# Gate and up of a routed expert with the weights stationary and 96 gathered tokens moving

## The chip, the cores and the metric

The kernel runs on one core of a Trainium2 chip. The metric is the device time of one execution in microseconds (us). The engines that matter are TensorE (PE, with its weight loads shown apart as PEld), VectorE (DVE), ScalarE (ACT) and SyncE (SP), which issues the DMAs.

## The reference

A decoder trunk of two layers runs over 256 tokens of width 1024, in float32. Layer 0 is an attention and retention mixer and a dense SwiGLU; layer 1 is another mixer and a mixture of eight experts, of which each token takes two. The change lies in the experts:

```python
logits = (xf @ router).astype(jnp.float32)            # 256 x 8
top_logits, top_idx = lax.top_k(logits, TOP_K)        # TOP_K = 2
gates = jax.nn.softmax(top_logits, axis=-1)
...
def expert_block(args):
    xb, e = args
    return (jax.nn.silu(xb @ w_gate[e]) * (xb @ w_up[e])) @ w_down[e]
```

`w_gate` and `w_up` are 1024 x 3584 for each expert and `w_down` is 3584 x 1024. The 256 tokens make 512 routed rows, 64 for an expert on the mean. With the reference's own default inputs its routing gives the eight experts 49, 66, 46, 70, 69, 61, 86 and 65 tokens.

## The kernel before

**Three products for one.** Each operand of a large product is split into a rounded part (`_hi`, type float32r) and the rest (`_lo`). `mm3` (lines 262 to 266) issues three matmuls into the same bank: hi x hi, hi x lo or lo x hi, and the other. The first operand of `mm3` is the stationary one, which a weight load puts into the array; the second one moves, at most 512 columns.

**Units.** Weights come in units of 128 x 1024 elements. SP loads two units at a time (1 MB) into one of 14 ring slots (`m_load`, line 1266). ACT rounds a unit into one of four buffers `w_hi` (`hi_unit`, line 273), DVE takes the rest into `w_lo` (`lo_unit`, line 277), and PE reads both. ACT may fill a buffer only when PE has finished the unit four before it (`unit_used`), and PE waits for `split_ready`, which DVE raises.

**Experts.** `moe_pe`, `moe_act`, `moe_dve` and `moe_sp` each loop over the eight experts. The hidden width of 3584 is cut into NFC = 7 chunks of 512. A chunk has 12 units: four of gate, four of up and four of down, so an expert has 84 and the eight have 672. PE's order in a chunk c from 1 on is gate(c), the turning of chunk c-1, up(c), down(c-1); gate and up of chunk 0 stand at the end of the expert before.

**Gathering.** For each expert `gather_pe` (line 1318) multiplies the normalised rows `xn` with a matrix `pick` of zeros and ones. That gives the expert's tokens transposed, with the width on the partitions: eight blocks of 128 x CAP, CAP = 128 being the number of places. ACT and DVE split them into `xe_hi` and `xe_lo`.

**Gate and up** (`gate_up`). The gathered tokens (128 x 128) are stationary and 512 columns of the weights move:

```python
for kk in range(2):
    k = 4 * plan[m][2] + 2 * u + kk
    w = slice(kk * 512, kk * 512 + 512)
    ins = mm3(bank, xe_hi[:, k, :], xe_lo[:, k, :], w_hi[:, buf, w], w_lo[:, buf, w],
              k == 0, k == KD - 1)
```

That is 6 matmuls for a unit. The product has the tokens on the partitions and the hidden width along the bank. ACT takes the silu of the gate (`silu_`, line 1347), DVE multiplies by up (`product`, line 1402), and since down contracts over the hidden width, `turn` transposes the result in four blocks on PE (line 1489) into bank 6. ACT rounds it (`turned`, line 1351) and DVE takes the rest (`rest`, line 1406).

**Down** (`down`). The turned block `hT` (128 x 128) is stationary and 512 columns of `w_down` move, 6 matmuls for a unit, summed over the chunks in banks 4 and 5. At the end of an expert the result is scaled by the gate and put back to its tokens by `scatter` (lines 1511 and 1512), and DVE adds it to `h` (line 1422).

**Order around the end of an expert.** On PE it is up(6), down(5), turning, the next expert's gather, down(6), gate(0) of the next expert, scatter, up(0).

**More tokens than places.** `overflow` reads the fullest expert's count on every engine, and if it is over CAP it runs the whole expert pass once more for the next CAP places.

**The dense SwiGLU of layer 0** is not touched. It has its weights stationary and 256 tokens moving (`f_gate_up`).

Of the kernel before, what the change touches and what calls it, by code (L numbers as in the profile page):

```python
# [26 lines left out]
P = 128  # L27
# [23 lines left out]
CAP = 128  # L51
# [17 lines left out]
def moe_items():  # L69
# [9 lines left out]
    ident=128, g_ab=8, eps=8, incl=128, negones=128, ones=128, before=128, strict=128, iota=256, cos_m=64, sin_m=64,  # L79
# [10 lines left out]
def trunk(nc, x, consts, decay_t, ab_w_in, w_uq, w_ukv, ab_w_out, f_gate, f_up, f_down,  # L90
          cd_w_in, cd_w_out, router, m_gate, m_up, m_down, moe_gain, final_gain, out):
    with ExitStack() as ctx:
# [70 lines left out]
        hT_lo = place("hT_lo", [P, 4, CAP], F32R, at=ARENA + 6144)  # L163
        g_moe_row = place("g_moe_row", [P, D], at=XT_AT + 12288)
        y_hi = place("y_hi", [P, D], F32R, at=ARENA + 8192)
        y_lo = place("y_lo", [P, D], F32R, at=XT_AT + 4096)
# [18 lines left out]
        def sem(name):  # L185
# [41 lines left out]
        prep_done, gather_banked, gather_hi, gathered, pgt_banked, pgt_done, e_silu, e_prod, h_banked, \  # L227
            hT_done, hT_lo_done, y_done, sc_banked, sc_done = (
                sem("e_" + n) for n in ("prep", "gather_banked", "gather_hi", "gathered", "pgt_banked",
                                        "pgt_done", "silu", "prod", "h_banked", "hT", "hT_lo", "y",  # L230
# [1071 lines left out]

        def gather_act(act, r, q):
            act.wait_ge(gather_banked, 2 * q + (r + 1))
            nc.scalar.activation(xe_hi[:, 4 * r:4 * r + 4, :].rearrange("p k t -> p (k t)"), pb[2 + r],
                                 ACT.Copy).then_inc(gather_hi, 1)

        def gather_dve(dve, r, q):
            dve.wait_ge(gather_hi, 2 * q + (r + 1))
            nc.vector.tensor_tensor(xe_lo[:, 4 * r:4 * r + 4, :].rearrange("p k t -> p (k t)"), pb[2 + r],  # L1310
                                    f32(xe_hi[:, 4 * r:4 * r + 4, :].rearrange("p k t -> p (k t)")),
                                    ALU.subtract).then_inc(gathered, 1)

        def gather_pe(pe, r):
            for kk in range(4):
                k = 4 * r + kk
                for tb in range(TB):
                    ins = nc.tensor.matmul(pb[2 + r][:, kk * P:kk * P + P], xn[:, tb, k * P:k * P + P],  # L1318
                                           pick[:, tb, :], start=tb == 0, stop=tb == 1)
            ins.then_inc(gather_banked, 1)  # L1320
# [21 lines left out]
        def moe_act(act, part):  # L1342
            def silu_(c, q):
                act.wait_ge(*m_used("g", c, q))

                act.wait_ge(h_banked, 7 * q + max(c, 1))
                nc.scalar.activation(eh[c % 2], pb[2 * (c % 2)], ACT.Silu).then_inc(e_silu, 1)

            def turned(c, q):
                act.wait_ge(h_banked, 7 * q + (c + 2))  # L1350
                nc.scalar.activation(hT_hi.rearrange("p j t -> p (j t)"), pb[6], ACT.Copy).then_inc(hT_done, 1)

            def outputs(q):
                act.wait_ge(*m_used("d", LAST, q))
                act.wait_ge(sc_done, 4 * q + 4)
                act.wait_ge(pgt_done, q + 1)
                for n in range(2):
                    nc.scalar.activation(y_hi[:, n * 512:n * 512 + 512], pb[4 + n], ACT.Copy,
                                         scale=place_gate).then_inc(y_hi_done, 1)

            def expert(e, q, last):
                for c in range(1, NFC):
                    m_hi(act, ("g", c), q)
                    m_hi(act, ("u", c), q)
                    turned(c - 1, q)
                    if c == 1:
                        act.wait_ge(pgt_banked, q + 1)

                        nc.scalar.activation(gate_sums, pb[7][:, 0:256], ACT.Copy,
                                             accum_out=place_gate).then_inc(pgt_done, 1)  # L1370
# [3 lines left out]
                turned(LAST, q)  # L1374
# [12 lines left out]
            q0 = NE * part  # L1387
            if part:
                m_hi(act, ("g", 0), q0)
            for r in range(2):  # L1390
                gather_act(act, r, q0)
            m_hi(act, ("u", 0), q0)
            silu_(0, q0)
            with act.Fori(0, NE - 1) as e:
                expert(e, e + q0, False)
            expert(NE - 1, q0 + NE - 1, True)

        def moe_dve(dve, part):
            def product(c, q):
                dve.wait_ge(*m_used("u", c, q))  # L1400
                dve.wait_ge(e_silu, 7 * q + (c + 1))
                nc.vector.tensor_tensor(eh[c % 2], eh[c % 2], pb[2 * (c % 2) + 1], ALU.mult).then_inc(e_prod, 1)

            def rest(c, q):
                dve.wait_ge(hT_done, 7 * q + (c + 1))
                nc.vector.tensor_tensor(hT_lo.rearrange("p j t -> p (j t)"), pb[6],  # L1406
                                        f32(hT_hi.rearrange("p j t -> p (j t)")),
                                        ALU.subtract).then_inc(hT_lo_done, 1)

            def outputs_rest(q):  # L1410
                for n in range(2):
                    w = slice(n * 512, n * 512 + 512)
                    dve.wait_ge(y_hi_done, 2 * q + (n + 1))
                    ins = nc.vector.scalar_tensor_tensor(out=y_lo[:, w], in0=pb[4 + n], scalar=place_gate,
                                                         in1=f32(y_hi[:, w]), op0=ALU.mult, op1=ALU.subtract)
                ins.then_inc(y_done, 1)
# [7 lines left out]
            def expert(e, q, last):  # L1424
                for c in range(1, NFC):
# [8 lines left out]
                    if c == 1:  # L1434
                        dve.wait_ge(pgt_done, q + 1)
                        nc.vector.tensor_scalar(pickT.rearrange("p b t -> p (b t)"), pb[7][:, 0:256], 0.0, None,
                                                ALU.is_gt).then_inc(pickT_done, 1)
# [34 lines left out]
        def moe_pe(pe, part):  # L1472
            def gate_up(kind, c, q):
                bank = pb[2 * (c % 2) + (kind == "u")]
                for m, u, n, buf in m_units((kind, c)):
                    pe.wait_ge(split_ready, UPE * q + (U_MOE + n + 1))
                    for kk in range(2):
                        k = 4 * plan[m][2] + 2 * u + kk
                        w = slice(kk * 512, kk * 512 + 512)
                        ins = mm3(bank, xe_hi[:, k, :], xe_lo[:, k, :], w_hi[:, buf, w], w_lo[:, buf, w],  # L1480
                                  k == 0, k == KD - 1)
                    ins.then_inc(unit_used, 1)

            def turn(c, q):
                pe.wait_ge(e_prod, 7 * q + (c + 2))
                if c:
                    pe.wait_ge(hT_lo_done, 7 * q + c)
                for j in range(4):
                    ins = nc.tensor.transpose(pb[6][:, j * P:j * P + P], eh[c % 2][:, j * P:j * P + P],  # L1489
                                              const("ident"))  # L1490
                ins.then_inc(h_banked, 1)

            def down(c, q):
                pe.wait_ge(hT_lo_done, 7 * q + (c + 1))
                if c == 0:
                    pe.wait_ge(y_done, q + 1)
                for m, u, n, buf in m_units(("d", c)):
                    t = 2 * plan[m][2] + u
                    pe.wait_ge(split_ready, UPE * q + (U_MOE + n + 1))
                    for nn in range(2):  # L1500
                        w = slice(nn * 512, nn * 512 + 512)
                        ins = mm3(pb[4 + nn], hT_hi[:, t, :], hT_lo[:, t, :], w_hi[:, buf, w],
                                  w_lo[:, buf, w], c == 0 and t == 0, c == LAST and t == 3)
                    ins.then_inc(unit_used, 1)

            def scatter(q):
                pe.wait_ge(y_done, q + 2)
                pe.wait_ge(pickT_done, q + 1)
                for s in range(4):
                    w = slice((s % 2) * 512, (s % 2) * 512 + 512)  # L1510
                    nc.tensor.matmul(pb[SC_BANKS[s]], pickT[:, s // 2, :], y_hi[:, w], start=True, stop=False)  # L1511
                    nc.tensor.matmul(pb[SC_BANKS[s]], pickT[:, s // 2, :], y_lo[:, w], start=False,  # L1512
                                     stop=True).then_inc(sc_banked, 1)

            def expert(q, last):
                for c in range(1, NFC):
# [4 lines left out]
                    turn(c - 1, q)  # L1521
                    if c == 1:
                        pe.wait_ge(prep_done, 2 * q + 2)
                        for tb in range(TB):
                            ins = nc.tensor.transpose(pb[7][:, tb * P:tb * P + P], pick_g[:, tb, :],
# [4 lines left out]
                turn(LAST, q)  # L1530
# [121 lines left out]
        def overflow(eng, body):  # L1652
# [3 lines left out]
            with eng.If(most > CAP):  # L1656
                body(eng, 1)
# [123 lines left out]
        def _(pe):  # L1781

            pe.sem_inc(unit_used, NBUF)
            pe.sem_inc(h_banked, 1)
# [17 lines left out]
        def _(dve):  # L1802
# [3 lines left out]
            dve.sem_inc(e_prod, 1)  # L1806
            dve.sem_inc(sc_done, 4)
# [34 lines left out]
def shape_tables(np):  # L1842
# [11 lines left out]
    t["iota"] = np.broadcast_to(np.arange(256, dtype=f), (P, 256))  # L1854
# [63 lines left out]
```

## Time and profile before

| | before |
|---|---|
| times of two runs | 1677.81 and 1678.82 us, median 1678.32 |
| span of the profiled execution | 1677.2 us, 0.6 and 1.6 us under the two times |
| PE busy | 1608.9 us (96%) |
| PEld busy | 1368.3 us (82%) |
| DVE busy | 1263.4 us (75%) |
| ACT busy | 1115.4 us (67%) |
| DMA | 444.35 MB, mean 265 GB/s |

The span runs from the first instruction to the last. Busy time of matmuls is longer than the step from one start to the next, since matmuls are pipelined and their ends are modelled: the price of a matmul in a stream is read from the starts in the timeline. PEclk is the clock granted to TensorE as a share of 2.4 GHz: 1.00 is 2.4 GHz, 0.50 is 1.2 GHz. The experts take the stretch from about 657 us to 1662 us.

### The profile page before, as it was taken

How to read it: one execution, taken by the hardware profiler on the slowest of the kernel's cores; microseconds unless marked ns; L12 is line 12 of the kernel's file. 1: busy time of each engine (PE TensorE's matmuls, PEld its weight loads, DVE VectorE, ACT ScalarE, POOL GpSimd, SP SyncE). 2: the span in 40 equal slices, each digit the busy share in tenths (PEclk: the TensorE clock that was granted, in tenths of full speed). 3: DMA queues.
4: the chain of work that ended last, by engine and by line, in shares of the span. 5: the costliest groups of instructions: out<-in, count | busy, mean ns of one | idle time of the engine just before them, and what ended most of it. 6: DMA issues, size and time to landing. Idle time of an engine off the chain costs nothing.

```text
span 1677.2 us, 23757 instructions
## 1 busy us (share of the span) xinstructions
PE 1608.9 (96%) x8136; PEld 1368.3 (82%) x8136; DVE 1263.4 (75%) x1430; ACT 1115.4 (67%) x1348; POOL 0.2 (0%) x4
## 2 busy tenths in 40 slices
PE   7988989999998998999999999999999999999995
PEld 6867789999898777888888888888888888888884
DVE  4446554445554556998998999999999999999995
ACT  5534454444365864887787787887877877877874
POOL 0000000000000000000000000000000000000000
PEclk9996999999998788999999999999999999999998
DMA  9630355554356054999999999999999999999950
GB/s 327 197 129 1 118 184 180 196 176 150 137 167 236 1 206 159 349 387 329 354 380 329 349 382 331 355 369 339 352 379 322 371 370 319 364 379 321 376 202 27
DMA packets 190916, 444.35 MB, mean 265 GB/s; under 512 B 7952, under 2 KB 25232, under 8 KB 190608
## 3 DMA queue, kind: packets, MB, share of 16 engines
q1 hardware_dynamic: 190864, 443.68, 73.6%
q8 instruction: 29, 0.48, 0.1%
q14 instruction: 23, 0.19, 0.0%
HBM read 442.61 MB, written 1.05 MB: 265 GB/s over the span
## 4 chain that ended last, share of the span: by engine, by line
PE 93%; DVE 3%; ACT 2%; issue 1%; DMA 0%; DVEq 0%; ACTq 0%; SPq 0%
PE bank L264 28%; PE bank L266 27%; PE bank L265 27%; PE bank L1318 2%; PE bank L1489 1%; PE bank L537 1%; PE bank L431 1%; PE bank L528 1%; PE bank L833 0%; ACT p_sb L593 0%; PE bank L1511 0%; PE bank L840 0%; PE bank L1512 0%; PE bank L527 0%; PE bank L418 0%
## 5 line engine op out<-in xcount | busy, mean ns | idle before, releaser
L277 DVE TENSOR_TENSOR w_lo<-ring,w_hi 128x1024 fp32r<-128x1024 f32 (+2 forms) x844 | 1004.9, 1208 | 272.2 <-ACT w_hi L273 233.1
L273 ACT ACTIVATE w_hi<-ring 128x1024 fp32r<-128x1024 f32 (+2 forms) x844 | 881.4, 1049 | 399.9 <-PE bank L266 398.5
L264 PE MATMUL bank<-w_hi,xe_hi 128*128 128x512 f32 x896 | 354.4, 396 | 1.4 <-DVE xe_lo L1310 1.4
L266 PE MATMUL bank<-w_hi,xe_lo 128*128 128x512 f32 x896 | 350.3, 391 | 0.0
L265 PE MATMUL bank<-w_lo,xe_hi 128*128 128x512 f32 x896 | 349.1, 390 | 0.0
L264 PEld LDWEIGHTS bank<-w_hi,xe_hi 128*128 128x128 f32 x896 | 168.3, 188 | 37.2 <-DVE w_lo L277 1.9
L266 PEld LDWEIGHTS bank<-w_hi,xe_lo 128*128 128x128 f32 x896 | 168.2, 188 | 36.3
L265 PEld LDWEIGHTS bank<-w_lo,xe_hi 128*128 128x128 f32 x896 | 168.4, 188 | 34.1
L264 PE MATMUL bank<-w_hi,hT_hi 128*128 128x512 f32 x448 | 177.9, 397 | 1.4 <-DVE hT_lo L1406 1.4
L266 PE MATMUL bank<-w_hi,hT_lo 128*128 128x512 f32 x448 | 176.9, 395 | 0.0
L265 PE MATMUL bank<-w_lo,hT_hi 128*128 128x512 f32 x448 | 176.8, 395 | 0.0
L264 PE MATMUL bank<-xT_hi,w_hi 128*128 128x256 f32 x448 | 127.0, 284 | 0.0
L265 PE MATMUL bank<-xT_lo,w_hi 128*128 128x256 f32 x448 | 126.9, 283 | 0.0
L266 PE MATMUL bank<-xT_hi,w_lo 128*128 128x256 f32 x448 | 126.8, 283 | 0.0
L264 PEld LDWEIGHTS bank<-w_hi,hT_hi 128*128 128x128 f32 x448 | 84.4, 188 | 20.8 <-DVE hT_lo L1406 1.6
L266 PEld LDWEIGHTS bank<-w_hi,hT_lo 128*128 128x128 f32 x448 | 84.4, 188 | 20.0
L265 PEld LDWEIGHTS bank<-w_lo,hT_hi 128*128 128x128 f32 x448 | 84.6, 189 | 19.3
L264 PE MATMUL bank<-w_hi,xT_hi 128*128 128x468 f32 (+1 forms) x256 | 90.4, 353 | 4.5 <-DVE w_lo L277 4.1
L265 PE MATMUL bank<-w_lo,xT_hi 128*128 128x468 f32 (+1 forms) x256 | 90.1, 352 | 0.0
L266 PE MATMUL bank<-w_hi,xT_lo 128*128 128x468 f32 (+1 forms) x256 | 90.1, 352 | 0.0
L264 PEld LDWEIGHTS bank<-xT_hi,w_hi 128*128 128x128 f32 x448 | 86.2, 192 | 0.2
L265 PEld LDWEIGHTS bank<-xT_lo,w_hi 128*128 128x128 f32 x448 | 86.1, 192 | 0.2
(246 smaller groups left out, 1672.0 us busy)
## 6 DMA issues: line engine op xcount, KB each, us to landing
ring<-m_gate_dram SPq DMA_DIRECT2D x112, 1024.0 KB, 6.3
ring<-m_up_dram SPq DMA_DIRECT2D x112, 1024.0 KB, 6.5
ring<-m_down_dram SPq DMA_DIRECT2D x112, 1024.0 KB, 6.2
ring<-ab_w_in_dram SPq DMA_DIRECT2D x16, 936.0 KB, 6.0
ring<-f_gate_dram SPq DMA_DIRECT2D x14, 1024.0 KB, 5.1
ring<-f_up_dram SPq DMA_DIRECT2D x14, 1024.0 KB, 5.1
ring<-f_down_dram SPq DMA_DIRECT2D x14, 1024.0 KB, 4.8
ring<-cd_w_in_dram SPq DMA_DIRECT2D x16, 704.0 KB, 4.2
```

Source lines behind the costliest of these rows:

```text
L264: nc.tensor.matmul(out_, a_hi, b_hi, start=first, stop=False, **kw)
L265: nc.tensor.matmul(out_, a_hi, b_lo, start=False, stop=False, **kw)
L266: return nc.tensor.matmul(out_, a_lo, b_hi, start=False, stop=last, **kw)
L273: nc.scalar.activation(w_hi[:, buf, 0:width], src, ACT.Copy).then_inc(hi_ready, 1)
L277: nc.vector.tensor_tensor(w_lo[:, buf, 0:width], src, f32(w_hi[:, buf, 0:width]), ALU.subtract).then_inc(split_ready, 1)
L431: ins = nc.tensor.transpose(pb[MIX_BANKS[b]][:, kk * 256 + tb * P:kk * 256 + tb * P + P], src[:, tb, k * P:k * P + P], const("ident"))
L528: nc.tensor.matmul(pb[i % 2][:, P:384], q[:, P:256], k[:, 0:256], start=True, stop=True).then_inc(s_banked, 1)
L537: ins = nc.tensor.transpose(pb[self.turn_banks[i % len(self.turn_banks)]][:, b * P:b * P + P], p_sb[i % 2][:, b * P:b * P + P], const("ide ...
L1318: ins = nc.tensor.matmul(pb[2 + r][:, kk * P:kk * P + P], xn[:, tb, k * P:k * P + P], pick[:, tb, :], start=tb == 0, stop=tb == 1)
L1489: ins = nc.tensor.transpose(pb[6][:, j * P:j * P + P], eh[c % 2][:, j * P:j * P + P], const("ident"))
```

## The change

CAP becomes 96 and PARTS = 3, so that three passes of 96 places cover 256 tokens; `overflow` runs parts 1 and 2 where an expert has more than 96 tokens. In gate and up the weights become stationary, in blocks of 128 columns, and the 96 gathered tokens move. Their product comes out with the hidden width on the partitions, as down wants it, so `turn`, bank 6's use for it and the semaphore `h_banked` go. The product is rounded from SBUF. In down the 96 tokens are stationary. The hi and lo parts of `hT` are doubled.

```diff
-CAP = 128
+CAP = 96
+PARTS = -(-256 // CAP)
...
-        xe_hi = place("xe_hi", [P, KD, CAP], F32R, at=XT_AT)
-        xe_lo = place("xe_lo", [P, KD, CAP], F32R, at=XT_AT + 8192)
-        eh = [place(f"eh{i}", [P, FC], at=ARENA + 2048 * i) for i in range(2)]
-        hT_hi = place("hT_hi", [P, 4, CAP], F32R, at=ARENA + 4096)
+        xe = place("xe", [P, KD, 2, CAP], F32R, at=XT_AT)
+        eh = [place(f"eh{i}", [P, 4, CAP], at=ARENA + 1536 * i) for i in range(2)]
+        hT_hi = [place(f"hT_hi{i}", [P, 4, CAP], F32R, at=ARENA + 3072 + 1536 * i) for i in range(2)]
...
             def silu_(c, q):
                 act.wait_ge(*m_used("g", c, q))
-                act.wait_ge(h_banked, 7 * q + max(c, 1))
-                nc.scalar.activation(eh[c % 2], pb[2 * (c % 2)], ACT.Silu).then_inc(e_silu, 1)
-
-            def turned(c, q):
-                act.wait_ge(h_banked, 7 * q + (c + 2))
-                nc.scalar.activation(hT_hi.rearrange("p j t -> p (j t)"), pb[6], ACT.Copy).then_inc(hT_done, 1)
+                act.wait_ge(hT_lo_done, 7 * q + c)
+                nc.scalar.activation(eh[c % 2].rearrange("p j t -> p (j t)"), pb[2 * (c % 2)][:, 0:4 * CAP],
+                                     ACT.Silu).then_inc(e_silu, 1)
+
+            def rounded(c, q):
+                act.wait_ge(e_prod, 7 * q + (c + 2))
+                if c >= 2:
+                    act.wait_ge(*m_used("d", c - 2, q))
+                else:
+                    act.wait_ge(unit_used, UPE * q + (U_MOE + NBUF))
+                nc.scalar.activation(hT_hi[c % 2], eh[c % 2], ACT.Copy).then_inc(hT_done, 1)
...
                     for kk in range(2):
                         k = 4 * plan[m][2] + 2 * u + kk
-                        w = slice(kk * 512, kk * 512 + 512)
-                        ins = mm3(bank, xe_hi[:, k, :], xe_lo[:, k, :], w_hi[:, buf, w], w_lo[:, buf, w],
-                                  k == 0, k == KD - 1)
+                        for j in range(4):
+                            w = slice(kk * 512 + j * P, kk * 512 + j * P + P)
+                            out_ = bank[:, j * CAP:j * CAP + CAP]
+                            ins = mm3(out_, w_hi[:, buf, w], w_lo[:, buf, w], xe[:, k, 0, :], xe[:, k, 1, :],
+                                      k == 0 and j == 0, k == KD - 1 and j == 3)
                     ins.then_inc(unit_used, 1)

-            def turn(c, q):
-                pe.wait_ge(e_prod, 7 * q + (c + 2))
-                if c:
-                    pe.wait_ge(hT_lo_done, 7 * q + c)
-                for j in range(4):
-                    ins = nc.tensor.transpose(pb[6][:, j * P:j * P + P], eh[c % 2][:, j * P:j * P + P],
-                                              const("ident"))
-                ins.then_inc(h_banked, 1)
-
             def down(c, q):
-                pe.wait_ge(hT_lo_done, 7 * q + (c + 1))
+                pe.wait_ge(hT_lo_done, 7 * q + (c + 2))
...
-                        ins = mm3(pb[4 + nn], hT_hi[:, t, :], hT_lo[:, t, :], w_hi[:, buf, w],
-                                  w_lo[:, buf, w], c == 0 and t == 0, c == LAST and t == 3)
+                        ins = mm3(pb[4 + nn][0:CAP, :], hT_hi[c % 2][:, t, :], hT_lo[c % 2][:, t, :],
+                                  w_hi[:, buf, w], w_lo[:, buf, w], c == 0 and t == 0, c == LAST and t == 3)
...
             with eng.If(most > CAP):
-                body(eng, 1)
+                for part in range(1, PARTS):
+                    body(eng, part)
```

## Rows read from the trace of the kernel before

**Rows 1.** The page: busy time, and the chain that ended last.
```profile
PE 1608.9 (96%) x8136; PEld 1368.3 (82%) x8136; DVE 1263.4 (75%) x1430; ACT 1115.4 (67%) x1348; POOL 0.2 (0%) x4
...
PE 93%; DVE 3%; ACT 2%; issue 1%; DMA 0%; DVEq 0%; ACTq 0%; SPq 0%
```

**Rows 2.** Stretches: us, busy (x) of PE, PEld, DVE, ACT, POOL, PEclk, DMA share, GB/s.
```profile
922.00:1043.00 121.00, 121.00 (x560) 99.84 (x560) 111.69 (x107) 96.28 (x103) 0.00 (x0) 1.00 0.97 352
...
999.00:1015.00 16.00, 16.00 (x72) 13.03 (x71) 14.75 (x15) 12.76 (x14) 0.00 (x0) 1.00 1.03 373
```

**Rows 3.** Timeline of PE, one chunk: start us, us, engine, line.
```profile
997.94 0.60 PE L1489 MATMUL bank<-cst,eh 128*128 128x128 f32 x4
...
1011.28 0.39 PE L266 MATMUL bank<-w_hi,xe_lo 128*128 128x512 f32 x1
...
1014.00 0.39 PE L266 MATMUL bank<-w_hi,xe_lo 128*128 128x512 f32 x1
...
1014.92 0.60 PE L1489 MATMUL bank<-cst,eh 128*128 128x128 f32 x4
```

**Rows 4.** Timeline of PE: four steps of down.
```profile
781.69 0.39 PE L265 MATMUL bank<-w_lo,hT_hi 128*128 128x512 f32 x1
...
782.62 0.39 PE L266 MATMUL bank<-w_hi,hT_lo 128*128 128x512 f32 x1
```

**Rows 5.** Timeline of PE: short matmuls in a stream at PEclk 1.00 (router, gather, values).
```profile
647.21 4.00 PE L1571 MATMUL bank<-router_sb,xT 128*128 128x8 f32 x32
...
777.88 3.74 PE L1318 MATMUL bank<-pick,xn 128*128 128x128 f32 x32
...
590.32 0.39 PE L545 MATMUL bank<-proj,pT_sb 128*128 128x64 f32 x2
590.54 0.39 PE L546 MATMUL bank<-proj,pT_sb 128*128 128x64 f32 x2
```

**Rows 6.** Timeline of PE: the dense SwiGLU, 13 steps with 256 columns moving.
```profile
402.37 0.28 PE L264 MATMUL bank<-xT_hi,w_hi 128*128 128x256 f32 x1
...
403.93 0.28 PE L265 MATMUL bank<-xT_lo,w_hi 128*128 128x256 f32 x1
```

**Rows 7.** Weight loads by line: xcount, ns min/median/max, first and last start.
```profile
L1571 PEld LDWEIGHTS bank<-router_sb,xT x32: 190/192/338, 647.1 to 650.8; 128*128 128x128 f32 x32
...
L266 PEld LDWEIGHTS bank<-w_hi,xe_lo x873: 187/188/188, 680.3 to 1642.9; 128*128 128x128 f32 x175
```

**Rows 8.** Timeline of PE at PEclk 0.50: 64 columns moving.
```profile
570.13 0.64 PE L1066 MATMUL bank<-proj,sb_a 128*128 128x64 f32 x2
570.56 0.63 PE L1067 MATMUL bank<-proj,sb_a 128*128 128x64 f32 x2
```

**Rows 9.** Stretches as in rows 2: before and after the clock fell or rose.
```profile
647.50:650.00 2.50, 2.50 (x24) 2.50 (x24) 1.86 (x5) 2.47 (x5) 0.00 (x0) 1.00 0.05 10
650.50:651.00 0.50, 0.50 (x4) 0.50 (x3) 0.00 (x0) 0.50 (x2) 0.00 (x0) 0.50 0.00 0
...
536.00:552.00 16.00, 16.00 (x60) 12.90 (x61) 8.14 (x20) 12.47 (x27) 0.00 (x0) 0.50 0.00 1
...
657.40:660.40 3.00, 2.97 (x14) 3.00 (x15) 3.00 (x3) 0.00 (x0) 0.00 (x0) 0.50 0.00 0
661.00:662.50 1.50, 1.50 (x16) 1.50 (x14) 1.50 (x2) 0.58 (x1) 0.00 (x0) 1.00 0.92 229
```

**Rows 10.** Timeline of PE at PEclk 0.50: 512 columns moving.
```profile
173.99 0.63 PE L265 MATMUL bank<-w_lo,mixT_hi 128*128 128x512 f32 x1
...
174.84 0.63 PE L264 MATMUL bank<-w_hi,mixT_hi 128*128 128x512 f32 x1
```

**Rows 11.** Groups by line, experts' stretch: xcount, busy us, mean ns, idle before.
```profile
L277 DVE TENSOR_TENSOR w_lo<-ring,w_hi 128x1024 fp32r<-128x1024 f32 x658 | 792.6, 1224 | 64.9 <-ACT w_hi L273 26.1
...
L1406 DVE TENSOR_TENSOR hT_lo<-bank,hT_hi 128x512 fp32r<-128x512 f32 x55 | 37.7, 685 | 1.0
L1402 DVE TENSOR_TENSOR eh<-eh,bank 128x512 f32<-128x512 f32 x55 | 37.4, 680 | 0.0
```

**Rows 12.** DMA issues: xcount, KB each, us to landing.
```profile
ring<-m_gate_dram SPq DMA_DIRECT2D x112, 1024.0 KB, 6.3
```

More of the change, by code:

```diff
@@ L78 @@
 CONST_WIDTHS = dict(
-    ident=128, g_ab=8, eps=8, incl=128, negones=128, ones=128, before=128, strict=128, iota=256, cos_m=64, sin_m=64,
+    ident=128, g_ab=8, eps=8, incl=128, negones=128, ones=128, before=128, strict=128, iota=PARTS * CAP, cos_m=64, sin_m=64,
     cos_r=128, sin_r=128, causal=384, dist=384, sb_neg=384, lower8=64, g_lat=5, g_mix=12,
@@ L157, in trunk @@
                   for j, n in enumerate(("abs", "sp", "t", "a"))]
-        xe_hi = place("xe_hi", [P, KD, CAP], F32R, at=XT_AT)
-        xe_lo = place("xe_lo", [P, KD, CAP], F32R, at=XT_AT + 8192)
-        eh = [place(f"eh{i}", [P, FC], at=ARENA + 2048 * i) for i in range(2)]
-        hT_hi = place("hT_hi", [P, 4, CAP], F32R, at=ARENA + 4096)
-        hT_lo = place("hT_lo", [P, 4, CAP], F32R, at=ARENA + 6144)
+        xe = place("xe", [P, KD, 2, CAP], F32R, at=XT_AT)
+        eh = [place(f"eh{i}", [P, 4, CAP], at=ARENA + 1536 * i) for i in range(2)]
+        hT_hi = [place(f"hT_hi{i}", [P, 4, CAP], F32R, at=ARENA + 3072 + 1536 * i) for i in range(2)]
+        hT_lo = [place(f"hT_lo{i}", [P, 4, CAP], F32R, at=(XT_AT + 6144, ARENA + 6144)[i]) for i in range(2)]
         g_moe_row = place("g_moe_row", [P, D], at=XT_AT + 12288)
         y_hi = place("y_hi", [P, D], F32R, at=ARENA + 8192)
-        y_lo = place("y_lo", [P, D], F32R, at=XT_AT + 4096)
+        y_lo = place("y_lo", [P, D], F32R, at=XT_AT + 8192)
         gate_sums = place("gate_sums", [P, 256], at=CONST_OFF + 4 * CONST_AT["cos_m"] // 32 * 32 + 32)
@@ L226, in trunk @@
         pick_done, y_hi_done, pickT_done = (sem(n) for n in ("pick_done", "y_hi_done", "pickT_done"))
-        prep_done, gather_banked, gather_hi, gathered, pgt_banked, pgt_done, e_silu, e_prod, h_banked, \
+        prep_done, gather_banked, gather_hi, gathered, pgt_banked, pgt_done, e_silu, e_prod, \
             hT_done, hT_lo_done, y_done, sc_banked, sc_done = (
                 sem("e_" + n) for n in ("prep", "gather_banked", "gather_hi", "gathered", "pgt_banked",
-                                        "pgt_done", "silu", "prod", "h_banked", "hT", "hT_lo", "y",
+                                        "pgt_done", "silu", "prod", "hT", "hT_lo", "y",
                                         "sc_banked", "sc_done"))
@@ L1317, in gather_pe @@
                 for tb in range(TB):
-                    ins = nc.tensor.matmul(pb[2 + r][:, kk * P:kk * P + P], xn[:, tb, k * P:k * P + P],
+                    ins = nc.tensor.matmul(pb[2 + r][:, kk * CAP:kk * CAP + CAP], xn[:, tb, k * P:k * P + P],
                                            pick[:, tb, :], start=tb == 0, stop=tb == 1)
@@ L1357, in outputs @@
                 for n in range(2):
-                    nc.scalar.activation(y_hi[:, n * 512:n * 512 + 512], pb[4 + n], ACT.Copy,
-                                         scale=place_gate).then_inc(y_hi_done, 1)
+                    nc.scalar.activation(y_hi[0:CAP, n * 512:n * 512 + 512], pb[4 + n][0:CAP, :], ACT.Copy,
+                                         scale=place_gate[0:CAP, :]).then_inc(y_hi_done, 1)
             def expert(e, q, last):
@@ L1364, in expert @@
                     m_hi(act, ("u", c), q)
-                    turned(c - 1, q)
+                    rounded(c - 1, q)
                     if c == 1:
                         act.wait_ge(pgt_banked, q + 1)
-                        nc.scalar.activation(gate_sums, pb[7][:, 0:256], ACT.Copy,
-                                             accum_out=place_gate).then_inc(pgt_done, 1)
+                        nc.scalar.activation(gate_sums[0:CAP, :], pb[7][0:CAP, 0:256], ACT.Copy,
+                                             accum_out=place_gate[0:CAP, :]).then_inc(pgt_done, 1)
                     silu_(c, q)
@@ L1373, in expert @@
                 m_hi(act, ("d", LAST), q, slice(0, 3))
-                turned(LAST, q)
+                rounded(LAST, q)
                 m_hi(act, ("d", LAST), q, slice(3, 4))
@@ L1413, in outputs_rest @@
                     dve.wait_ge(y_hi_done, 2 * q + (n + 1))
-                    ins = nc.vector.scalar_tensor_tensor(out=y_lo[:, w], in0=pb[4 + n], scalar=place_gate,
-                                                         in1=f32(y_hi[:, w]), op0=ALU.mult, op1=ALU.subtract)
+                    ins = nc.vector.scalar_tensor_tensor(out=y_lo[0:CAP, w], in0=pb[4 + n][0:CAP, :],
+                                                         scalar=place_gate[0:CAP, :], in1=f32(y_hi[0:CAP, w]),
+                                                         op0=ALU.mult, op1=ALU.subtract)
                 ins.then_inc(y_done, 1)
@@ L1435, in expert @@
                         dve.wait_ge(pgt_done, q + 1)
[L1436 to L1437 removed]
+                        nc.vector.tensor_scalar(pickT[0:CAP].rearrange("p b t -> p (b t)"), pb[7][0:CAP, 0:256],
+                                                0.0, None, ALU.is_gt).then_inc(pickT_done, 1)
                     if c == 1 and not last:
@@ L1510, in scatter @@
                     w = slice((s % 2) * 512, (s % 2) * 512 + 512)
-                    nc.tensor.matmul(pb[SC_BANKS[s]], pickT[:, s // 2, :], y_hi[:, w], start=True, stop=False)
-                    nc.tensor.matmul(pb[SC_BANKS[s]], pickT[:, s // 2, :], y_lo[:, w], start=False,
+                    nc.tensor.matmul(pb[SC_BANKS[s]], pickT[0:CAP, s // 2, :], y_hi[0:CAP, w], start=True, stop=False)
+                    nc.tensor.matmul(pb[SC_BANKS[s]], pickT[0:CAP, s // 2, :], y_lo[0:CAP, w], start=False,
                                      stop=True).then_inc(sc_banked, 1)
@@ L1806, in _ @@
             dve.sem_inc(e_prod, 1)
+            dve.sem_inc(hT_lo_done, 1)
             dve.sem_inc(sc_done, 4)
@@ L1853, in shape_tables @@
     t["strict"] = (row < col).astype(f)
-    t["iota"] = np.broadcast_to(np.arange(256, dtype=f), (P, 256))
+    t["iota"] = np.broadcast_to(np.arange(PARTS * CAP, dtype=f), (P, PARTS * CAP))
     def rotary(half):
```

21 lines of the change are left out of this document (9 added, 12 removed).

## The prediction

> **What bounds the kernel now.** I read the page first: PE is busy for 96% of the span and carries 93% of the chain [rows 1]. Then I read the stretches: through the experts PE has no idle time and full clock, 2.4 GHz, while DVE is busy for 111.7 of 121 us and the DMA queues for 97% [rows 2]. So PE's own stream sets the time, and DVE and the DMAs follow within a tenth. The timeline gives PE's prices: from turning to turning a chunk takes 1014.92 - 997.94 = 16.98 us, and twelve matmuls of gate take 2.72 us, 0.2267 each [rows 3]; in down four steps take 0.93 us, 0.233 each [rows 4]. A chunk is 48 x 0.2267 = 10.88 us of gate and up, 24 x 0.233 = 5.59 of down, and 0.51 that is left for the turning with its change of operands. There are 7 x 8 = 56 chunks.
>
> **Removed.** The turning: 0.51 us x 56 = 29 us of PE. ACT's and DVE's waits for it go with it; neither is on the path.
>
> **Gate and up.** A chunk's 48 matmuls of 512 columns become 192 of 96 columns. The moving columns fall by a quarter, 24,576 to 18,432, but each matmul now brings a new 128 x 128 weight block for 96 columns. The price of such a matmul is the step that decides. No float32r matmul in this trace moves fewer than 256 columns, so I bound it from both sides.
>
> - Below: with nothing but columns to pay for, 96 columns are 0.040 us. The SwiGLU's 256 columns (0.1067 us at 2.4 GHz) take 1.56 / 13 = 0.120 [rows 6], 0.013 over; the same surplus on 96 gives 0.053.
> - Middle: float32 matmuls with other column counts and a full weight block each. Of 128 columns, 32 rows take 3.74 us, that is (3.74 - 0.275) / 31 = 0.112 (0.275 is one matmul's duration in this group). Of 64 columns, two rows take 0.22, that is 0.11. Of 8 columns, 32 take 4.00 us, about 0.12, with the clock down at the end [rows 5]. A sixteenth of the columns saves nothing: what is paid is the weight block. The float32r weight loads last as long as the router's (188 ns against 192) [rows 7], so the float32r block should cost the same 0.11.
> - Above: a short float32r matmul could be run as a float32 one, which the trace shows as two rows each: 2 x 0.112 = 0.224.
>
> I take 0.110, the row it is nearest to by weight block and by load. At full clock gate and up take 192 x 0.110 = 21.1 us for a chunk, against 10.88.
>
> TensorE: Matmul & The Clock Gate of the Trainium skill (section Back-to-back issue gap) states about 81 ns for a sustained stream of loads and matmuls of 128 columns. The rows above give 0.112 at 128 columns, so they disagree; by the page a chunk's gate and up would be 15.6 us and the kernel about 1910.
>
> **The clock.** At 1.2 GHz the same 64-column pairs take 0.43 us, 0.2133 for one [rows 8], and a 512-column matmul takes 0.85 / 2 = 0.427 [rows 10]. Which clock will be granted? While the router's 8-column matmuls were issued back to back, with no idle time, the clock stood at 1.00 up to 650.0 and was 0.50 from 650.5 on [rows 9]; the stream had begun at 647.2, and 3.1 us later it fell. So matmuls that mostly load weights don't hold it. From 536 to 552 PE was never idle, with attention's short matmuls, and stayed at 0.50 all the time. The 128-column float32 gather rose from 0.50 to 1.00 within some 3.2 us [rows 9]. The new gate and up lie between the router's stream and the gather's: for most of its 0.11 us a matmul has no column moving. I expect the clock to fall in each gate-and-up stretch and to come back in each down, where 512 columns move in each matmul.
>
> A chunk is then: gate and up, 3.1 us at full clock (28 matmuls) and 164 x 0.2133 = 35.0, together 38.1 us; down, 3.2 us at half clock (7.5 matmuls) and 16.5 x 0.233 = 3.8, together 7.0. That is 45.1 us against 16.98, 28.1 more. Times 56 it is 1575 us, in which the turning's gain is counted. Both lags may be longer: 5 us each make it 1523.
>
> **The rest, costed at nothing.** ACT's silu and rounding and DVE's product and rest shrink from 512 to 384 columns. A chunk of DVE is 12 x 1.224 + 0.685 + 0.680 = 16.05 us [rows 11], far inside 45; so are the 6 MB of loads. `rounded` stands behind up's four roundings on ACT, in front of silu, and reads SBUF; it and `rest` must end before down(c-1), behind up(c), which now lasts 19 us. If that cover went, down would wait for both a chunk, about 2 x 0.68 = 1.4 us by DVE's row, 76 us in all. SP's and DVE's queues keep their order. The gather keeps its weight blocks and so its 3.7 us; the scatter keeps its 512 columns. Of `overflow` nothing runs: the trace has 112 loads of gate, which is eight experts by 14 [rows 12], so no expert has more than 128 tokens, and by the reference's routing the fullest has 86, below 96.
>
> **Sum.** 1677.2 + 1575 = 3252 for the span; the median of the runs is 1.1 above it. With the longer lags, 3200. I say 3250; this case's own range is 3100 to 3350.
>
> **Rivals.**
>
> 1. The clock stays at 2.4 GHz. A chunk is 21.1 + 5.6 = 26.7 us, 9.7 more, 545 in all: 2222. For it: the SwiGLU's stationary weights run at full clock, and PE never idles. Against it: neither did it in the router's stream when the clock fell. The Trainium skill (same page, section What's actually happening) ties the low clock to how busy the PE has recently been and warns of idle gaps; there are none here, so by it this rival would hold, but the router's row speaks against it. Chance 0.14.
> 2. The float32r weight block loads faster than the float32 one, so that columns are paid and not blocks: 192 x 0.053 = 10.2 us and 15.8 for a chunk on PE. Then DVE's 16.05 binds (the DMAs would have to carry 6.29 MB in it, 392 GB/s, against 373 in rows 2): 0.93 us x 56 = 52 less, 1625. This is the case on the other side; it decides below (10.88 + 0.51) / 192 = 0.059 us a matmul. For it: no row prices a short float32r matmul. Against it: the equal loads of rows 7. The same page (Weight-path perf modes) states that a fast weight load is on for 128 weights where the dtype isn't FP32, which a float32r block might meet. Chance 0.14, of which 0.03 leaves the gain inside 2%, lost to DVE and the DMAs.
> 3. Short float32r matmuls run as float32 ones do: 192 x 0.224 = 43.0, a chunk of 48.6, 31.6 more, 3447; if only the columns are paid four times (4 x 0.040 = 0.160), 2760. The clock holds, since columns move for most of the time. Chance 0.13.
> 4. The clock doesn't come back in down either: 192 x 0.2133 + 24 x 0.427 = 51.2, 34.2 more, 1916, and 32 x 0.10 + 8 x 0.2 = 4.8 for each of eight gathers and scatters, 38: 3630. Chance 0.09.
> 5. Something between, such as the page's 81 ns at full clock (1910), or extra passes after all: 0.04.
>
> **How the numbers follow.** The forecast has 0.46. From 2200 to 3650 the range holds cases 1, 3, 4 and the forecast, 0.82; it leaves out case 2 and most of 5. Two per cent is about what a measurement can tell from no change. Faster by more than 2%: 0.12 (case 2 and a little of 5 less what is lost to DVE). Within: 0.03. Slower: 0.85.
>
> **What will show it.** The step between starts of gate's matmuls: 0.11 where PEclk is 1.00, 0.213 where it is 0.50, and weight loads that last 188 ns and about 335. PEclk in the chunks: 1.00 at the beginning of a gate stretch, then 0.50, and 1.00 in the second half of down; a mean near 0.6 over the experts. No L1489 rows. DVE and the DMAs well under half busy. The forecast is wrong if gate's stretches show 1.00 throughout (case 1), if the weight loads are shorter than before (case 2), if a gate matmul shows as two rows (case 3), or if loads of gate number more than 112.

## The result and the profile after

The changed kernel takes 3208.22 us (median of two runs, 3206.05 and 3210.38) against 1678.32: the ratio is 1.912, 95% interval 1.907 to 1.917. The profiled execution has a span of 3204.3 us.

The page of the changed kernel, as in [rows 1]:

```profile
PE 3133.2 (98%) x15976; PEld 2937.4 (92%) x15976; DVE 1264.0 (39%) x1430; ACT 1107.4 (35%) x1348; POOL 0.2 (0%) x4
...
PE 96%; ACT 2%; DVE 2%; issue 1%; DMA 0%; DVEq 0%; ACTq 0%; SPq 0%
```

PE is still the bound, more so than before. DVE and ACT do the same work in twice the time. The stretches of one chunk and the beginning of the next one, with the columns of [rows 2] (us, busy and count of PE, PEld, DVE, ACT, POOL, then PEclk, DMA share, GB/s):

```profile
1981.60:2001.60 20.00, 20.00 (x96) 20.00 (x95) 5.37 (x5) 5.13 (x8) 0.00 (x0) 0.50 0.32 105
2001.90:2004.70 2.80, 2.80 (x8) 1.90 (x9) 1.47 (x2) 1.06 (x1) 0.00 (x0) 0.50 0.00 0
2005.00:2008.90 3.90, 3.90 (x18) 2.74 (x17) 3.54 (x8) 2.97 (x3) 0.00 (x0) 1.00 0.78 255
2008.90:2015.10 6.20, 6.20 (x58) 6.19 (x56) 3.59 (x3) 2.81 (x3) 0.00 (x0) 1.00 0.88 295
2015.30:2046.00 30.70, 30.70 (x141) 30.10 (x141) 8.49 (x8) 7.29 (x9) 0.00 (x0) 0.50 0.34 111
```

PE has no idle time in any of them. Up ends at 2001.9 at half clock. Down starts there at half clock, and its steps shorten from 0.43 to 0.23 us at 2004.97, 3.1 us later. The next gate, from 2008.91 on, keeps the full clock for 6.3 us, and then it is at 0.50 until the next down. The first two rows' DMA share against 0.97 before shows the queues waiting for PE. The same stretch in the timeline of PE (start us, us, engine, line):

```profile
2001.91 0.70 PE L264 MATMUL bank<-w_hi,hT_hi 128*96 128x512 f32 x1
...
2003.27 0.63 PE L264 MATMUL bank<-w_hi,hT_hi 128*96 128x512 f32 x1
2003.69 0.63 PE L265 MATMUL bank<-w_lo,hT_hi 128*96 128x512 f32 x1
...
2009.07 0.28 PE L266 MATMUL bank<-xe,w_lo 128*128 128x96 f32 x1
...
2015.10 0.31 PE L266 MATMUL bank<-xe,w_lo 128*128 128x96 f32 x1
...
2015.64 0.41 PE L266 MATMUL bank<-xe,w_lo 128*128 128x96 f32 x1
2015.85 0.41 PE L264 MATMUL bank<-xe,w_hi 128*128 128x96 f32 x1
```

Between 2009.07 and 2015.10 lie 54 steps: 0.1117 us each at full clock. At half clock a step is 0.2134 (2015.64 to 2017.77 are ten). A step of down takes 0.42 to 0.43 at half clock. The next down starts at 2044.01, which makes this chunk 42.1 us long, against 16.98 in [rows 3].

The weight load of gate and up at full clock, and the transposing of the gates, once an expert:

```profile
2009.02 0.19 PEld L266 LDWEIGHTS bank<-xe,w_lo 128*128 128x128 f32 x1
```

```profile
L1524 PE MATMUL bank<-cst,pick_g x16: 421/426/431, 716.2 to 2928.1; 128*96 128x128 f32 x16
```

The load lasts as long as in [rows 7]. Line 1524 runs once an expert. From its first to its eighth start, 716.2 to 2928.1, are seven experts, 316.0 us each; line 1525 of the kernel before, the same transposing, ran from 681.2 to 1552.8, 124.5 each. The difference, 191.5 x 8 = 1532 us, is the whole of what the span grew by (1527).

### The profile page after: what moved, and what is told of

Same layout as the page of the kernel before. It is cut to its first block, busy times and chain, and to the rows that moved or that the text cites. A ratio compares the mean times of both kernels' runs of the same rounds, so it can differ in the third digit from the quotient of the medians.

```text
span 3204.3 us, 39445 instructions
## 1 busy us (share of the span) xinstructions
PE 3133.2 (98%) x15976; PEld 2937.4 (92%) x15976; DVE 1264.0 (39%) x1430; ACT 1107.4 (35%) x1348; POOL 0.2 (0%) x4
## 4 chain that ended last, share of the span: by engine, by line
PE 96%; ACT 2%; DVE 2%; issue 1%; DMA 0%; DVEq 0%; ACTq 0%; SPq 0%
PE bank L264 30%; PE bank L265 30%; PE bank L266 30%; PE bank L1319 1%; PE bank L1511 0%; PE bank L1512 0%; ACT p_sb L593 0%; PE bank L431 0%; PE bank L833 0%; ACT L593 0%; PE bank L840 0%; PE bank L418 0%; DVE h L508 0%; PE bank L537 0%; DMA h<-x_dram 0%
## 5 line engine op out<-in xcount | busy, mean ns | idle before, releaser
L266 PE MATMUL bank<-xe,w_lo 128*128 128x96 f32 x3584 | 1377.6, 384 | 0.0
L265 PE MATMUL bank<-xe,w_hi 128*128 128x96 f32 x3584 | 1375.9, 384 | 0.0
L264 PE MATMUL bank<-xe,w_hi 128*128 128x96 f32 x3584 | 1369.1, 382 | 1.8 <-DVE xe L1312 1.2
L264 PEld LDWEIGHTS bank<-xe,w_hi 128*128 128x128 f32 x3584 | 1089.1, 304 | 6.5 <-DVE xe L1312 1.3
L265 PEld LDWEIGHTS bank<-xe,w_hi 128*128 128x128 f32 x3584 | 1091.5, 305 | 2.9
L266 PEld LDWEIGHTS bank<-xe,w_lo 128*128 128x128 f32 x3584 | 1094.0, 305 | 0.0
L264 PE MATMUL bank<-w_hi,hT_hi 128*96 128x512 f32 x448 | 218.0, 487 | 1.5 <-DVE hT_lo L1413 1.5
L265 PE MATMUL bank<-w_lo,hT_hi 128*96 128x512 f32 x448 | 210.5, 470 | 0.0
L266 PE MATMUL bank<-w_hi,hT_lo 128*96 128x512 f32 x448 | 207.0, 462 | 0.0
L264 PEld LDWEIGHTS bank<-w_hi,hT_hi 128*96 128x96 f32 x448 | 93.8, 209 | 40.9 <-DVE hT_lo L1413 2.0
L266 PEld LDWEIGHTS bank<-w_hi,hT_lo 128*96 128x96 f32 x448 | 89.8, 201 | 43.9
L265 PEld LDWEIGHTS bank<-w_lo,hT_hi 128*96 128x96 f32 x448 | 91.5, 204 | 37.6
```

The lines of the kernel that those rows point to most:

```text
L264: nc.tensor.matmul(out_, a_hi, b_hi, start=first, stop=False, **kw)
L265: nc.tensor.matmul(out_, a_hi, b_lo, start=False, stop=False, **kw)
L266: return nc.tensor.matmul(out_, a_lo, b_hi, start=False, stop=last, **kw)
```

## The experiments

The theory after the result has two parts. A float32r matmul with a new 128 x 128 weight block has a fixed price, unless its columns take longer: 0.2134 us at half clock, which is 256 cycles, and 0.1117 at full clock, which is 268. And this stream of 96 moving columns a block loses the full clock because so few columns move. The rivals: columns are paid; the clock falls for another reason (the array that is only partly used, the count of loads, idle time).

| run | us | PEclk in the experts | blocks and moving columns of gate and up, a chunk |
|---|---|---|---|
| before | 1678 | 1.00 | 48, 24,576 |
| after | 3208 | 0.59 | 192, 18,432 |
| old96 | 1671 | 1.00 | 48, 24,576 |
| cap64 | 3263 | 0.57 | 192, 12,288 |
| same_block | 3209 | 0.59 | 192, 18,432 |
| two_products | 2453 | 0.63 | 128, 12,288 |
| merged | 1953 | 0.91 | 134, 18,432 |
| cap128 | 2399 | 0.91 | 192, 24,576 |
| cap128_unrolled | 2240 | 1.00 | 192, 24,576 |
| fill1 | 2575 | 0.88 | 200, 22,528 |
| fill1_all | 2493 | 0.92 | 200, 22,528 |
| fill_unrolled | 2378 | 1.00 | 200, 22,528 |
| fill4 | 2904 | 0.89 | 224, 34,816 |
| cap128_fill | 2507 | 0.92 | 200, 28,672 |

PEclk is that of the stretch from 1000 to 1500 us, or of 664 to 2480 for fill1_all and cap128_fill. All but before, after and old96 are single times. Thirteen executions of the kernel before lay between 1673.67 and 1683.31 us, 0.6% apart, so differences of some per cent can be read from single times.

**old96: the operands as before, only 96 places.** The kernel before with CAP and PARTS changed and 96 of 128 partitions or columns where tokens stand:

```diff
-CAP = 128
+CAP = 96
...
-                        ins = mm3(bank, xe_hi[:, k, :], xe_lo[:, k, :], w_hi[:, buf, w], w_lo[:, buf, w],
+                        ins = mm3(bank[0:CAP, :], xe_hi[:, k, :], xe_lo[:, k, :], w_hi[:, buf, w], w_lo[:, buf, w],
```

> The kernel before with CAP = 96 alone: 96 gathered tokens stationary, 512 columns of the weights moving, the turning kept, three parts in the general path. Theory (the loss is all in exchanging the operands): PE's stream is the same 504 matmuls of 512 columns for an expert, so 1678 us within 0.5%, granted clock 1.00 in the experts. Rival (a stationary operand of 96 columns lets the clock fall or costs on its own): the clock is below 1.00 in some chunks and the time is over 1700.

1670.78 us over ten runs, ratio 0.9949, interval 0.9933 to 0.9965. The whole loss lies in the exchange of operands, none of it in 96 places. A stationary operand of 96 columns, in gate and up and in down, didn't cost the clock either: 1.00 in the experts. That it is half a per cent faster than before has no cause shown in the experts: a chunk takes 16.99 us (976.49 to 993.48, the turnings' starts) as before. In its profile the first gather starts at 652.4 instead of 657.4, so the gain lies ahead of the experts, where only the place of the constants differs; why, stays open. It is the fastest of the versions run.

**cap64 and same_block: fewer columns, and the same block twice.** cap64 sets CAP = 64 and leaves the general path out, so tokens beyond the 64th of an expert are missing. same_block changes the order of the three products:

```diff
-                            ins = mm3(out_, w_hi[:, buf, w], w_lo[:, buf, w], xe[:, k, 0, :], xe[:, k, 1, :],
-                                      k == 0 and j == 0, k == KD - 1 and j == 3)
+                            nc.tensor.matmul(out_, w_hi[:, buf, w], xe[:, k, 0, :], start=k == 0 and j == 0, stop=False)
+                            nc.tensor.matmul(out_, w_hi[:, buf, w], xe[:, k, 1, :], start=False, stop=False)
+                            ins = nc.tensor.matmul(out_, w_lo[:, buf, w], xe[:, k, 0, :], start=False,
+                                                   stop=k == KD - 1 and j == 3)
```

> The changed kernel with 64 gathered tokens moving in gate and up instead of 96, and no general path: the tokens of an expert beyond the 64th are left out. Theory (a matmul pays for its weight block, 256 cycles of the granted clock): the steps stay 0.111 at full clock and 0.213 at half clock, the clock falls as before, about 3200 us within 2%. Rival (columns are paid): two thirds of the gate and up time, 0.142 a step at half clock, about 2500 us.

> The changed kernel with the products in the order w_hi x hi, w_hi x lo, w_lo x hi, so that the same weight block stands twice in a row. Theory (each matmul loads its block, the same or not): 3208 us within 2%, steps 0.111 and 0.213. Rival (a block that is already there isn't paid again): every third step falls to the columns' 0.08 at half clock, 20% less gate and up time, about 2700 us.

3262.8 and 3209.3 us. A third fewer columns made nothing faster; the step is the same (timeline of cap64, ten steps in 2.13 us):

```profile
1500.11 0.40 PE L264 MATMUL bank<-xe,w_hi 128*128 128x64 f32 x1
...
1502.24 0.40 PE L265 MATMUL bank<-xe,w_hi 128*128 128x64 f32 x1
```

The 1.7% more fit its lower clock, 0.57 against 0.59. In same_block a block that is already in the array is paid again. The rivals of both runs fall.

**cap128: a third more columns.** CAP = 128, with the buffers moved to fit:

```diff
-CAP = 96
+CAP = 128
```

> The changed kernel with 128 gathered tokens moving in gate and up instead of 96 (general path of two parts). Theory (weight block paid): the steps stay 0.111 and 0.213; if the clock behaves as with 96, 3208 us within 2%; if 128 columns in each matmul are enough to hold it, about 2230 us. Rival (columns are paid): 0.284 a step at half clock, about 4000 us.

2398.8 us, between the two numbers of the theory (3208 and 2230) and far below after. The step at full clock is 0.1115 with 128 columns too, so moving a third more costs nothing. But the clock is not 1.00 throughout. The timeline and the stretches of one expert's end:

```profile
1101.86 0.28 PE L266 MATMUL bank<-xe,w_lo 128*128 128x128 f32 x1
1106.46 0.47 PE L264 MATMUL bank<-xe,w_hi 128*128 128x128 f32 x1 [4.32 <-issue]
```

```profile
1106.50:1150.00 43.50, 43.50 (x199) 43.08 (x200) 10.03 (x9) 9.82 (x12) 0.00 (x0) 0.50 0.27 95
1155.00:1300.00 145.00, 145.00 (x1140) 138.37 (x1139) 86.07 (x79) 75.08 (x78) 0.00 (x0) 1.00 0.68 233
```

For 4.32 us PE had no instruction ("issue": no wait that the profile shows); this is where its loop over the experts jumps back. The clock falls within this gap (1.00 from 1102.2 to 1104.8, 0.50 from 1104.9 to 1106.4) and stays at 0.50 through gate and up of chunk 1, until down. The second row is most of the rest of the expert, with its downs. In gate and up of these two rows the same stream of 128 columns a matmul stays at whichever of the two clocks it had.

**merged and two_products: as few blocks, with more and with fewer columns.** merged moves the hi and the lo part past one w_hi block; the second half lands in spare columns of the bank and is left out of the result. two_products leaves the product w_hi x lo out altogether.

```diff
+                            both = bank[:, j * CAP:j * CAP + (5 - j) * CAP].rearrange(
+                                "p (s t) -> p s t", t=CAP)[:, ::4 - j, :]
+                            if k or not j:
+                                nc.tensor.matmul(both, w_hi[:, buf, w], xe[:, k, :, :],
+                                                 start=k == 0, stop=False)
...
+                            ins = nc.tensor.matmul(out_, w_lo[:, buf, w], xe[:, k, 0, :], start=False,
+                                                   stop=k == KD - 1 and j == 3)
```

> The changed kernel with two of the three products of gate and up in one matmul: w_hi is loaded once and 192 columns, the hi and the lo part of the tokens, move past it; the lo products are gathered in spare columns of the bank and left out of the result. 134 weight blocks in a chunk instead of 192, moving columns nearly the same (18,624 against 18,432). Theory (block paid, clock follows the columns): at the least 30% less time in gate and up, so about 2525 us if the clock still falls, and about 1880 us if it holds at 1.00. Rival (columns are paid): 3208 us within 2%.

> The changed kernel without the product of w_hi and the lo part of the tokens in gate and up: 128 matmuls of 96 columns in a chunk. The count of weight blocks is nearly that of merged (134), but a third fewer columns move. Theory (the block is paid and the clock follows the columns that move): the clock falls again, steps 0.111 and 0.213, a chunk of some 30 us, about 2400 us. Rival (the clock fell because of the number of loads or matmuls): with as few as in merged it holds, about 1900 us.

1952.8 and 2453.5 us with nearly the same count of blocks. (What was expected of merged counts 18,624 moving columns; its 3248 matmuls of 192 columns and 4256 of 96 make 18,432 a chunk, exactly those of after.) merged has the full clock for most of the time, two_products alternates as after does:

```profile
1200.00:1262.00 62.00, 62.00 (x481) 57.01 (x480) 47.16 (x43) 40.81 (x43) 0.00 (x0) 1.00 0.90 309
```

```profile
1000.00:1500.00 500.00, 495.13 (x2462) 458.48 (x2462) 255.23 (x245) 214.86 (x232) 0.00 (x0) 0.63 0.58 198
```

The first row is merged, the second two_products. So the count of loads isn't what takes the clock. That merged is 4% over its 1880 goes with the place where PE's loop jumps back, as in cap128: PE is without an instruction for 1.6 to 1.9 us there, six times, and behind each the clock is at 0.50 for 27.3 us, until the next down. That is some 6 x (1.8 + 27.3 / 2) = 93 us (an estimate; merged wasn't run with the loop written out):

```profile
1145.86 0.35 PE L1492 MATMUL bank<-xe,w_hi 128*128 128x192 f32 x1 [1.78 <-issue]
```

```profile
1146.00:1147.60 1.60, 1.60 (x16) 1.60 (x16) 0.90 (x2) 0.00 (x0) 0.00 (x0) 1.00 0.92 332
1147.80:1173.00 25.20, 25.20 (x121) 25.19 (x120) 9.04 (x8) 8.54 (x11) 0.00 (x0) 0.50 0.46 162
```

In merged a matmul of 192 columns and one of 96 take together what two blocks take, 0.22 us (1202.60 to 1202.82):

```profile
1202.60 0.32 PE L1492 MATMUL bank<-xe,w_hi 128*128 128x192 f32 x1
1202.75 0.23 PE L1497 MATMUL bank<-xe,w_lo 128*128 128x96 f32 x1
1202.82 0.32 PE L1492 MATMUL bank<-xe,w_hi 128*128 128x192 f32 x1
```

**fill1 and fill4: more work, less time.** Matmuls of 512 columns into an idle bank are added, their results unused; fill1 has one in a unit (`% 8 == 7`), fill4 four (`% 2 == 1`), and up of chunk 0 has none.

```diff
+                            if (4 * kk + j) % 8 == 7 and (kind, c) != ("u", 0):
+                                nc.tensor.matmul(pb[6], w_hi[:, buf, w], w_hi[:, buf, 0:512],
+                                                 start=True, stop=True)
                             ins = mm3(out_, w_hi[:, buf, w], w_lo[:, buf, w], xe[:, k, 0, :], xe[:, k, 1, :],
                                       k == 0 and j == 0, k == KD - 1 and j == 3)
```

> The changed kernel with one matmul of 512 columns into an idle bank added to each unit of gate and up (but not in up of chunk 0), its result unused. At full clock the additions are 8 x 0.23 us a chunk, about 100 us in all. Theory (more moving columns hold the clock): if one in 25 is enough, 2340 us; if it isn't, the clock falls as before and the additions cost up to 0.43 each, 3300 us. Rival (the clock doesn't depend on moving columns): 3300 us.

> The changed kernel with four matmuls of 512 columns into an idle bank added to each unit of gate and up (but not in up of chunk 0), their results unused: more work and nothing taken away. Theory (the clock follows the moving columns): granted clock near 1.00, a chunk of 8 x (24 x 0.111 + 4 x 0.233) + 5.6 = 34.5 us, about 2630 us, faster than without them. Rival (the clock doesn't depend on moving columns): the additions are paid at half clock too, 3700 us or more.

2575 and 2904 us: with nothing taken away, 633 and 304 us less than after. That is the clock, shown by itself: the same 192 blocks, PE busy for over 99% of the stretch in all three, and only matmuls added. Both missed the theory's number by 10%, since the clock fell once an expert. In fill1:

```profile
985.00:1155.00 170.00, 170.00 (x1315) 157.80 (x1314) 95.38 (x90) 80.37 (x87) 0.00 (x0) 1.00 0.65 220
1160.00:1215.00 55.00, 54.38 (x241) 52.39 (x241) 13.80 (x14) 12.01 (x15) 0.00 (x0) 0.50 0.29 97
```

Up of chunk 0, without additions, starts at 1152; at 1158.6 the clock falls, 6.7 us later, before any idle time. After that gate and up of chunk 1, which have the additions, stay at 0.50 until down: the additions hold the full clock but don't bring it back.

**fill1_all and cap128_fill: additions everywhere.**

```diff
-                            if (4 * kk + j) % 8 == 7 and (kind, c) != ("u", 0):
-                                nc.tensor.matmul(pb[6], w_hi[:, buf, w], w_hi[:, buf, 0:512],
+                            if (4 * kk + j) % 8 == 7:
+                                idle = pb[4] if (kind, c) == ("u", 0) else pb[6]
+                                nc.tensor.matmul(idle, w_hi[:, buf, w], w_hi[:, buf, 0:512],
```

> The kernel of fill1 with the added matmul in every unit of gate and up, up of chunk 0 included (there into bank 4). In fill1 the clock fell in that stretch alone and stayed at 0.50 until the next down. Theory: with nothing left out the clock holds at 1.00 through all experts, and a chunk is 8 x (24 x 0.1115 + 0.237) + 5.6 = 28.9 us: 2350 us. Rival (once an expert the clock falls for another reason, such as the short idle time at the loop's restart): 2575 us within 2%.

> The kernel of cap128 with one added 512-column matmul in every unit of gate and up. cap128 held the clock but for one stretch of about 50 us an expert, which began with 4.3 us in which PE had no instruction. Theory (the idle time lets the clock fall and 128 columns a matmul don't bring it back): the added columns bring it back sooner, at full clock 2350 us, and up to 100 us more for what the idle time still costs. Rival (additions are only more work): 2500 us or more.

2492.6 and 2506.9 us. The rival of fill1_all was right: up of chunk 0 now keeps the clock, but PE reaches the jump back at full speed, idles for about 4 us there (the profile puts most of these gaps down to a wait for DVE's product at line 1409, one to "issue"; the version written out below tells which), and the clock is at 0.50 for some 50 us. In cap128_fill the additions didn't bring it back sooner; they were only more work, as its rival had it.

**cap128_unrolled and fill_unrolled: no jump back.**

```diff
-            with pe.Fori(0, NE - 1) as e:
+            for e in range(NE - 1):
                 expert(e + q0, False)
```

> The kernel of cap128 with PE's loop over the experts written out, so that PE's program has no branch back; the other engines keep their loops. Theory (the 4.3 us without an instruction come from the jump back in a long loop body, and they alone let the clock fall): no such gap, granted clock 1.00 in the experts, 16.5 us less in gaps shown for four experts and 50 us at half clock less an expert: about 2220 us. Rival (the clock falls there for another reason, the scatter or up of chunk 0): the gaps go but the low stretches stay, 2370 us or more.

> The kernel of fill1_all with PE's loop over the experts written out. Theory: no gap at the restart, so the clock holds at 1.00 with 96 tokens and one added matmul in 25; a chunk is 28.9 us, 2350 us. Rival: 2490 us within 2%.

2240.3 and 2377.5 us, as the theory had it within 1.2%. The profile of cap128_unrolled:

```profile
664.00:2220.00 1556.00, 1552.48 (x12375) 1487.43 (x12373) 922.47 (x874) 785.81 (x827) 0.00 (x0) 1.00 0.64 217
```

So the gap and the low stretch behind it came from the jump back: with the same data waits and no jump neither is there. In cap128_unrolled gate and up run even from 867.6 to 899.8 us, where no down stands between them, at 1.00.

fill_unrolled had one low stretch, in its first expert, with no gap in it: gate began at 656.9 at full clock, the clock fell at 658.0, and down brought it back at 750.1. From there to 2300 the same stream with its additions ran at 1.00:

```profile
658.10:745.00 86.90, 86.90 (x394) 85.34 (x394) 19.55 (x19) 18.77 (x21) 0.00 (x0) 0.50 0.26 89
750.20:1000.00 249.80, 249.80 (x1944) 232.62 (x1942) 137.54 (x132) 116.78 (x124) 0.00 (x0) 1.00 0.63 216
```

fill1_all has the same matmuls there and ran them at 1.00. What let the clock fall in the one and not in the other is open.

## Why the prediction was right

The likeliest case came true: 3250 was said, 3208 measured, and the span was 48 us below its 3252. The mechanism held in both its parts; that the number came within 1.3% is partly luck, since its misses have both signs. By its steps:

- **The price of a short float32r matmul** was taken as 0.110 from the float32 rows and measured 0.1117 at full clock, 0.2134 at half clock against 0.2133 said. The reason given (what is paid is the block) is shown by cap64, cap128 and same_block. (In [rows 10] 0.85 / 2 is 0.425, not 0.427; nothing hangs on it.) The Trainium skill, TensorE: Matmul & The Clock Gate, section LDWEIGHTS, puts a load at its column count divided by 1.2, in ns, which is 107 for 128 columns. At full clock the measured step agrees within 5%; at half clock it nearly doubles, which that rule doesn't have. The fast weight load, which that page's section on weight-path modes ties to a dtype that isn't FP32, didn't show for float32r: its loads lasted 0.19 us, those of float32 192 ns [rows 7]. Nor did the 81 ns of its section Back-to-back issue gap, against a step of 0.1117 us.
- **The clock** alternated as said, with a mean of 0.59. That few moving columns are the cause was argued from the router's row, which couldn't show it alone: PE had idled for 1.4 us shortly before.

```profile
645.08 2.29 PE L418 MATMUL bank<-cst,h 128*128 128x128 f32 x16 [1.38 <-DVE h L508]
```

  two_products against merged, and fill1, show it.
- **The two lags** were taken as 3.1 and 3.2 us from a row each, and are the terms that were mis-sized. Over the experts the clock fell 3.5 to 6.8 us after down's end, 5.0 on the mean, and rose 2.3 to 5.6 us after its start, 4.0 on the mean (3.1 and 5.3 in the two chunks above; at 2049.21 the step goes from 0.43 to 0.28). A microsecond more at full clock saves 0.2134 / 0.1117 - 1 = 0.91 us. By the starts in the timeline gate and up took 2072 us in the experts, against 56 x 38.1 = 2134 said, and down 406 against 56 x 7.0 = 392. The two differences, 62 less and 14 more, make up the 48 us. The prediction's own variant with lags of 5 us each gave 3200.
- **A wrong picture of the expert's end**: the sum has a down, and so a return of the clock, behind each gate and up. But up of chunk 0 and gate and up of chunk 1 follow each other with no down between, and the clock has already fallen in the gate of chunk 0 ahead of them:

```profile
993.00:1054.70 61.70, 61.61 (x291) 61.44 (x289) 15.66 (x16) 12.77 (x15) 0.00 (x0) 0.50 0.32 103
```

  In six of the seven turns from one expert to the next these 61.7 us are at half clock throughout, and in the other one all but 3.4 us. The longer lags behind the other downs outweighed this.
- **The work around it** was hidden as said. DVE's and ACT's waits grew (DVE waited 1499 us for ACT's roundings, ACT 1650 for PE), and rounded and rest ended long before down. The expert's 316.0 us compare with 7 x 45.1 + 6 = 322.
- **The turning** is gone from the trace; its 29 us can't be told apart from the rest.
- **What wasn't seen**: the loop body of PE has so many instructions now that the jump back can leave PE without one for 4 us. In the changed kernel itself it hardly shows: PE's idle time for want of an instruction is 0.4 us over the experts, since it comes to the jump at half clock. Where the clock held (cap128, fill1_all, merged) it came up.

Of the rivals, case 1 (full clock) didn't happen in this kernel; cap128_unrolled, with more columns moving and no jump back, comes near to what it would have given: 2240 against the 2222 worked out. Case 2 is excluded: no run had a step below 0.11 a block. Case 3 is excluded, since each gate matmul is one row, and case 4, since the clock rose in every down that it hadn't risen before.

## What to carry to other kernels

Choose as stationary the operand whose blocks are used for many columns. Here one block for 96 columns costs as much as for 128, so the saved quarter of the columns bought four times the matmuls at 0.11 us instead of a step of 0.23. Compare the blocks at 0.11 us each with the time of their columns (0.23 us for 512), take the larger, and then read from a short run whether PE still has the full clock; here the second question cost more than the first (968 of 1530 us: 3208 to 2240). If work of PE is cut and its clock falls, added idle columns can cost less than the clock gives back, but the better answer is a larger moving operand (old96: 1671).

## What the runs showed of the hardware that was not expected

- The clock depends on what went before and not on the stream alone: cap128 stayed at 0.50 for 44 to 48 us after 4.3 us of idle time, in code that ran at 1.00 in cap128_unrolled; merged stayed there for 27 us after 1.8. fill_unrolled stayed at 0.50 for 92 us without a gap and then ran the same stream at 1.00 for 1600 us. In all of them it was down, with 512 columns a matmul, that brought the clock back.
- A jump back in a long loop on PE left it without an instruction for 4.3 us (cap128), 0.6 to 1.6 us when PE came to it at half clock (fill1). Written out, the program had no such gap.
- Adding one matmul of 512 columns to each 24 of 96 made the kernel 633 us faster.
